# A gated-recurrence layer on one core: the first score matmuls of each head in the middle of a weight piece, and operands 128 bytes lower

## The chip, the cores and the metric

The kernel runs on one core of a Trainium2 chip. The metric is the device time of one execution in microseconds (us). The core has five engines with instruction streams of their own: TensorE (PE: matmuls; its weight loads are listed as PEld), VectorE (DVE), ScalarE (ACT), GpSimd (POOL) and SyncE (SP, which issues most DMAs). They meet through semaphores only: an instruction may wait until a counter has a value, and may raise one when it ends.

## What is computed

One layer of a streaming encoder, for a prompt of 2048 frames and a sample of 64 frames with a state carried in; the model width is 1024. Layer 0 is the only layer, so of the four token mixers only HGRN2 (a gated linear recurrence) runs, followed by a SwiGLU channel mixer, each behind an RMSNorm and added to its input:

```python
def _gla_chunk(state, q, k, v, logf):          # one chunk of 64 frames of one head, 8 heads of 128
    G = jnp.cumsum(logf, axis=2)
    g_mid = G[:, :, L // 2][:, :, None]
    g_last = G[:, :, L - 1][:, :, None]
    scores = jnp.einsum('bhtd,bhsd->bhts', q * jnp.exp(G - g_mid), k * jnp.exp(g_mid - G))
    scores = jnp.where(tril, scores, 0.0)
    o = scores @ v + jnp.einsum('bhtd,bhdv->bhtv', q * jnp.exp(G), state)
    new_state = exp(g_last).T * state + einsum('bhsd,bhsv->bhdv', k * jnp.exp(g_last - G), v)

def _hgrn2(h, layer, state, w_in, lower_bounds, out_gain, w_out):
    q, f, i, g = jnp.split(h @ w_in, ...)      # 1024 -> 4 x 1024
    fg = lb + (1.0 - lb) * sigmoid(f); k = 1.0 - fg; logf = log(fg); v = i
    o, state = _chunked_scan(_gla_chunk, ...)
    o = _rmsnorm(o, out_gain)
    return (o * silu(g)) @ w_out, state

x = x + _hgrn2(rmsnorm(x)); x = x + (silu(gate) * up) @ w_down     # gate, up: 1024 -> 2816 each
```

## The kernel before

**Tiling.** The 2048 frames go through in four blocks. Block 0 has 512 prompt frames and the 64 sample frames (576, handled as two halves of 288 columns); blocks 1 to 3 have 512. Block 0 is written out, blocks 1 to 3 are one loop. All activations stand with the features on the 128 partitions and the frames along the row. Every large product is made of three matmuls on a high and a low part of each operand (`w_hi*h_hi + w_hi*h_lo + w_lo*h_hi`, lines 452 to 454 in `products`).

**A block** has three stages. (1) The eight heads: for each, q, f, i and g are projected from `h_hi`, `h_lo` by eight weight *pieces* of four 128-row tiles, that is 4 x 3 = 12 matmuls of 512 columns to a piece. (2) The output projection, from the heads' results `a_hi`, `a_lo`. (3) The SwiGLU: gate and up by a Strassen scheme (for each of 22 tiles seven operands, A11, S2, S3, S1, A22, A12, S4 in that order, of 4 x 3 matmuls of 256 columns: 1848 a block, 5544 in blocks 1 to 3; `strassen`, lines 544 to 546), and down, again from `a_hi`, `a_lo`, which by then hold the SwiGLU's products (22 x 8 x 3 = 528 matmuls of 512 columns a block, 1584 in blocks 1 to 3; the output projection has 576 there).

**Weights** arrive in a ring of four buffers, three pieces ahead. For each piece ACT makes `w_hi` (line 761) and DVE `w_lo` (line 941, `split_lo`), once the piece that used the buffer has been multiplied.

**The recurrence of head h-1 is woven into head h's pieces.** Behind piece u of head h, every engine runs its `recurrence(b, h - 1, u)`. A block's 512 frames are four *pairs* of chunks, p = 0 to 3. PE's steps are: `turn_values` (u = 0: v transposed into `ps_u`), `scores` of pair u into `ps_s`, `turn_keys` of pair u into `ps_k`, `update` of pair u-1 (state update), `outputs` of pair u-2. On the other engines: `keep_scores` (DVE, lines 964 and 965: two masked copies from `ps_s` to `sc`), `keys_by_frame` (ACT, line 662: `ps_k` to `kx`), `next_states` (DVE, line 988), `first_state` (DVE, line 973: `smid`).

**What waits for what.** There is one bank `ps_s` and one bank `ps_k`. So the scores of pair p wait until pair p-1 has been copied out:

```python
wait(pe, sc_ready, pair_no(b, h, p))      # in scores: for p > 0, behind keep_scores(p - 1)
pe.wait_ge(kx_ready, pair_no(b, h, p) + 1)     # in update(p): behind keys_by_frame(p)
```

The first pair's scores wait for q and k with their decays, of which `qe` (DVE, line 1108) is written last before them; `turn_keys(0)` waits for `kh` (line 1113). At each boundary between two heads, DVE also finishes an older head's output: `oscale` (line 996), `y` (line 1000), then ACT rounds it to `a_hi` (line 694, `y_part`), then DVE takes the rest as `a_lo` (line 1009, `y_part`). DVE runs in the order it is written in, with `y_part` behind `recurrence(b, h - 1, 0)` and ahead of the next `split_lo`. The boundary behind the first head of a block has no `y_part`. The eighth head's recurrence is woven into the first pieces of the output projection (`last_head`).

So a block has 8 places where a head's recurrence begins: a first one, six with `y_part`, and that of `last_head`.

**Addresses.** `place` hands out bytes of each partition in the order of the calls. `h_hi` begins at byte 16512, `h_lo` at 34944, `w_hi` at 107648, `w_lo` at 115840; then come small tables, of which `coef` (3 numbers for each of 4 pairs) is the last, and the next address is rounded up to 128. There `a_hi` begins, at 148992; `a_lo` at 167424, the gate and up weights `g_hi` at 200192 and `g_lo` at 214528, and behind them the scratch tensors of the heads that lie over these. The Strassen operands of the activations (`h2`, at 16512) have slots of 1152 bytes; with the weights' slots of 2048 bytes, an operand's address less its weight's leaves, modulo 512: 0 for A11 and S2, 128 for S3 and A12, 256 for A22 and S4, 384 for S1 (for the high parts). For `h_hi` less `w_hi` it leaves 0 modulo 128 and 0 modulo 256 (16512 - 107648 = -356 x 256); for `a_hi` less `w_hi` it leaves 128 modulo 256.

Of the kernel before, what the change touches and what calls it, by code (L numbers as in the profile page):

```python
# [19 lines left out]
P = 128  # L20
EPS = 1e-6
D = 1024
KT = D // P
HEADS = 8
# [35 lines left out]
PAIRS = TB // P  # L60
# [3 lines left out]
def hybrid_layer(nc, x_t, w_all, gain_mix, gain_ffn, bounds, out_gain, state_in, y_t, state_p, state_s,  # L64
# [3 lines left out]
    at = [-(-nc.sbuf_base // 32) * 32]  # L68

    def place(name, shape, dt=F32, offset=None):  # L70
        here = at[0] if offset is None else offset
        size = 4
        for n in shape[1:]:
            size *= n
        size = (size + 31) // 32 * 32
        if offset is None:
            at[0] += size
        return nc.alloc_sbuf_tensor_at(name, shape, dt, offset=here), here + size
# [22 lines left out]
    fbuf, _ = place("fbuf", [P, 2, T0])  # L101
    gmix, _ = place("gmix", [P, KT])
    gffn, _ = place("gffn", [P, KT])
    bnd, _ = place("bnd", [P, 2, HEADS])
    bexp, _ = place("bexp", [P, 2, HEADS])
    bmax, _ = place("bmax", [P, HEADS])
    bsum, _ = place("bsum", [P, HEADS])
# [3 lines left out]
    ogain, _ = place("ogain", [P, 1])  # L111
    eps, _ = place("eps", [P, 1])
    e_mid, _ = place("e_mid", [P, 2 * PAIRS + 2])
    coef, _ = place("coef", [P, PAIRS, 3])

    at[0] = -(-at[0] // P) * P
    a_at = at[0]
# [174 lines left out]
    with nc.Block() as block:  # L292

        @block.tensor
        def _(pe):
# [83 lines left out]
            def out_square_sum(b, h):  # L379
                if isinstance(h, int) and h == HEADS - 1:  # L380
                    pe.wait_ge(osq_ready, HEADS * b + h + 1)
                    mm = pe.matmul(ps_s[:, 0:TB], ones[:], osq[:, 0:TB], start=True, stop=True)
                    if first(b):
                        mm = pe.matmul(ps_k[:, 0:CH], ones[:], osq[:, TB:T0], start=True, stop=True)
                    mm.then_inc(oms_done, 1)
                    return
                pe.wait_ge(osq_lo_ready, HEADS * b + h + 1)
                pe.matmul(ps_s[:, 0:TB], ones_r[:], osq_hi[:, 0:TB], start=True, stop=False)
                mm = pe.matmul(ps_s[:, 0:TB], ones_r[:], osq_lo[:, 0:TB], start=False, stop=True)
                if first(b):  # L390
                    pe.matmul(ps_k[:, 0:CH], ones_r[:], osq_hi[:, TB:T0], start=True, stop=False)
                    mm = pe.matmul(ps_k[:, 0:CH], ones_r[:], osq_lo[:, TB:T0], start=False, stop=True)
                mm.then_inc(oms_done, 1)

            def recurrence(b, h, u):

                n = pairs_of(b)
                if u == 0:
                    turn_values(b, h)
                if u == VS_STEP and first(b):  # L400
                    turn_sample_values(b, h)
                if 0 <= u - 2 < n:
                    outputs(b, h, u - 2)
                if 0 <= u - 1 < n:
                    update(b, h, u - 1)
                if u < n:
                    scores(b, h, u)
                    turn_keys(b, h, u)
                if u == P_HEAD - 1:
                    out_square_sum(b, h)  # L410

            def slot_read(b, h, t, recur):

# [17 lines left out]
            def head(b, T, h, recur):  # L431

                for u in range(P_HEAD):
                    t, half = u // 2, u % 2
                    if not recur:
                        t, half = ((0, 0), (1, 0), (0, 1), (1, 1), (2, 0), (2, 1), (3, 0), (3, 1))[u]
                    if half == 0:
                        slot_read(b, h, t, recur)
                    piece(b, T, slot(b, t), P_HEAD * h + u, u % RING, half, KT, h_hi, h_lo,
                          KT * b if u in (0, 2) and not recur else None)  # L440
                    if recur:
                        recurrence(b, h - 1, u)
                    elif u == (2 if first(b) else 3):
                        norm_sum(b, T, 2 * b)
# [3 lines left out]
            def products(T, s, ring, kk, k, stop, part_hi, part_lo):  # L448
                for bank, c, n in halves(T):
                    o = ps[s % 2][:, s // 2 + bank, 0:n]  # L450
                    hh, hl = part_hi[:, k, c:c + n], part_lo[:, k, c:c + n]
                    pe.matmul(o, w_hi[:, ring, kk, :], hh, start=(k == 0), stop=False)  # L452
                    pe.matmul(o, w_hi[:, ring, kk, :], hl, start=False, stop=False)  # L453
                    last_mm[0] = pe.matmul(o, w_lo[:, ring, kk, :], hh, start=False, stop=stop)  # L454

            def piece(b, T, s, n, ring, j, tiles, part_hi, part_lo, part_wait=None):

                pe.wait_ge(w_lo_ready, PIECES * b + n + 1)
                for kk in range(min(KP, tiles - j * KP)):
                    k = j * KP + kk  # L460
                    if part_wait is not None:
                        pe.wait_ge(h_lo_ready, part_wait + k + 1)
                    products(T, s, ring, kk, k, k == tiles - 1, part_hi, part_lo)
                last_mm[0].then_inc(pieces_done, 1)

            def last_head(b, T):


                h = HEADS - 1


                pieces = ((0, 0), (1, 0), (0, 1), (1, 1), (2, 0), (3, 0))
                parts = [(n, m, KP * half + kk) for n, (m, half) in enumerate(pieces) for kk in range(KP)
                         if KP * half + kk < h and (m < 2 or not first(b))]
                share = (4, 1, 1, 1, 1, 1, 1, 1) if first(b) else (4, 2, 2, 2, 2, 1, 0, 1)
                for u in range(P_HEAD + 1):
                    take = share[u] if u < len(share) else len(parts)
                    for n, m, k in parts[:take]:
                        if k % KP == 0:
                            pe.wait_ge(w_lo_ready, PIECES * b + OUT0 + n + 1)  # L480
                        if k == 0:
                            if first(b):
                                pe.wait_ge((v_t_ready, qe_ready)[m], HEADS * (b + 1))
                            else:
                                pe.wait_ge((f_norm_ready, g_norm_ready, v_t_ready, qe_ready)[m], HEADS * (b + 1))
                        if n == 0 and k == 0:
                            pe.wait_ge(y_lo_ready, HEADS * b + h - 1)
                        if n == 2 and k == h - 1:
                            pe.wait_ge(y_lo_ready, HEADS * b + h)
                        products(T, slot(b, m), n % RING, k % KP, k, False, a_hi, a_lo)  # L490
                        if n < 2 and k == KP - 1:
                            last_mm[0].then_inc(pieces_done, 1)
                    parts = parts[take:]
                    if u < P_HEAD:
                        recurrence(b, h, u)
                pe.wait_ge(y_lo_ready, HEADS * (b + 1))
                for m in range(2):
                    products(T, slot(b, m), 2 + m, KP - 1, KT - 1, True, a_hi, a_lo)

                    last_mm[0].then_inc(pieces_done, 1 if first(b) or m == 0 else 3)  # L500
# [123 lines left out]
        def _(act):  # L624
# [71 lines left out]
            def recurrence(b, h, u):  # L696
                n = pairs_of(b)
                if u == 0:
                    values_by_frame(b, h)
                if u == VS_STEP and first(b):  # L700
                    sample_values_by_frame(b, h)
                if u < n:
                    keys_by_frame(b, h, u)
                if u == n + 1:
                    out_squares(b, h)
# [230 lines left out]
        def _(dve):  # L936
# [74 lines left out]
            def recurrence(b, h, u):  # L1011
                n = pairs_of(b)
                if u == 0:
                    first_state(b, h)
                if 0 <= u - 1 < n:
                    next_states(b, h, u - 1)
                if u < n:
                    keep_scores(b, h, u)
                if u == P_HEAD - 2 and (first(b) or (isinstance(h, int) and h == HEADS - 1)):
                    low_squares(b, h)  # L1020
# [311 lines left out]
            dve.wait_ge(x1_ready, 2)  # L1332
            nc.vector.tensor_copy(ones_r[:], ones[:]).then_inc(dve_const, 1)
            nc.vector.memset(e_mid[:, 2 * PAIRS:2 * PAIRS + 1], 1.0).then_inc(dve_const, 1)
            nc.vector.memset(coef[:, :, 2:3], 1.0).then_inc(dve_const, 1)
            dve.wait_ge(dve_const, 4)
            dve.wait_ge(dn_done, 2)
            for s in range(2):
                dve.wait_ge(y_stored[s], 1)
# [21 lines left out]
            nc.vector.tensor_scalar(oml[:], lb[:], -1.0, 1.0, ALU.mult, ALU.add).then_inc(bound_ready, 1)  # L1361
            dve.wait_ge(bound_step, 7)
            dve.wait_ge(bound_ready, 1)
            dve.wait_ge(smp_loaded, 16)
            block_program(0, T0)
            with dve.Fori(1, BLOCKS) as b:
# [335 lines left out]
```

## Time and profile before

| | |
|---|---|
| median of 3 runs | 2655.53 us (2654.55 to 2661.32) |
| the profiled execution | 2655.65 us; its span from first to last instruction 2653.9 us |
| granted TensorE clock, mean | 0.993 of full speed |
| busy: PE, DVE, ACT, POOL | 2579.9, 1795.3, 1237.2, 259.9 us |

A busy engine executes something; PE's busy time and the durations of its matmuls overlap (a matmul starts before the one ahead of it has drained), so what a matmul costs is read from start to start. The engine with the largest share sets the time as long as the others deliver to it in time; where it stands idle, the trace names what ended the wait.

### The profile page before, as it was taken

How to read it: one execution, taken by the hardware profiler on the slowest of the kernel's cores; microseconds unless marked ns; L12 is line 12 of the kernel's file. 1: busy time of each engine (PE TensorE's matmuls, PEld its weight loads, DVE VectorE, ACT ScalarE, POOL GpSimd, SP SyncE). 2: the span in 40 equal slices, each digit the busy share in tenths (PEclk: the TensorE clock that was granted, in tenths of full speed). 3: DMA queues.
4: the chain of work that ended last, by engine and by line, in shares of the span. 5: the costliest groups of instructions: out<-in, count | busy, mean ns of one | idle time of the engine just before them, and what ended most of it. 6: DMA issues, size and time to landing. Idle time of an engine off the chain costs nothing.

```text
span 2653.9 us, 52582 instructions
## 1 busy us (share of the span) xinstructions
PE 2579.9 (97%) x16420; PEld 2339.6 (88%) x16420; DVE 1795.3 (68%) x3025; ACT 1237.2 (47%) x2195; POOL 259.9 (10%) x196
## 2 busy tenths in 40 slices
PE   8999989999999999999999999999999999999998
PEld 7999989999988887998987887889897888799897
DVE  6666587877756677766656676766565676766565
ACT  5444454433444555443435555534344554644343
POOL 3111110000021112000011111100002111200001
PEclk9999999999999999999999999999999999999999
DMA  5322345645542224765753222667554222467574
GB/s 183 96 59 59 112 139 175 205 162 178 175 142 76 71 75 127 215 210 161 217 154 96 71 75 88 208 181 226 155 178 144 72 75 73 150 198 223 153 224 140
DMA packets 203408, 379.63 MB, mean 143 GB/s; under 512 B 23168, under 2 KB 23200, under 8 KB 203056
## 3 DMA queue, kind: packets, MB, share of 16 engines
q1 hardware_dynamic: 202896, 369.73, 45.1%
q0 software_dynamic: 384, 8.44, 0.9%
q8 instruction: 50, 0.82, 0.1%
q14 instruction: 78, 0.64, 0.1%
HBM read 331.67 MB, written 52.74 MB: 145 GB/s over the span
## 4 chain that ended last, share of the span: by engine, by line
PE 56%; DVE 8%; issue 6%; ACT 5%; DMA 0%; DVEq 0%; ACTq 0%; SPq 0%; POOL 0%; POOLq 0%
PE ps L452 9%; PE ps L454 9%; PE ps L453 9%; PE ps L544 8%; PE ps L546 8%; PE ps L545 8%; DVE w_lo L941 2%; PE ps_s L330 1%; PE ps_s L544 1%; PE ps_s L545 1%; PE ps_s L546 1%; ACT L729 1%; DVE gcum L1037 1%; ACT w_hi L761 1%; DVE coef L1093 1%
## 5 line engine op out<-in xcount | busy, mean ns | idle before, releaser
L544 PE MATMUL ps<-h,g_hi 128*128 128x256 f32 (+1 forms) x2112 | 608.8, 288 | 29.8 <-DVE xres L1131 9.7
L546 PE MATMUL ps<-h,g_lo 128*128 128x256 f32 (+1 forms) x2112 | 604.5, 286 | 0.0
L545 PE MATMUL ps<-h,g_hi 128*128 128x256 f32 (+1 forms) x2112 | 604.2, 286 | 0.0
L941 DVE TENSOR_TENSOR w_lo<-w_raw,w_hi 128x512 fp32r<-128x512 f32 x512 | 370.2, 725 | 235.8 <-ACT w_hi L761 234.4
L452 PE MATMUL ps<-h_hi,w_hi 128*128 128x512 f32 (+1 forms) x1280 | 470.9, 368 | 15.8 <-DVE h_lo L946 10.6
L761 ACT ACTIVATE w_hi<-w_raw 128x512 fp32r<-128x512 f32 x512 | 317.1, 624 | 334.7 <-PE ps L454 319.0
L454 PE MATMUL ps<-h_hi,w_lo 128*128 128x512 f32 (+1 forms) x1280 | 453.0, 354 | 0.0
L453 PE MATMUL ps<-h_lo,w_hi 128*128 128x512 f32 (+1 forms) x1280 | 451.8, 353 | 0.0
L452 PE MATMUL ps<-a_hi,w_hi 128*128 128x512 f32 (+1 forms) x1200 | 432.9, 361 | 6.1 <-DVE w_lo L941 3.5
L544 PEld LDWEIGHTS ps<-h,g_hi 128*128 128x128 f32 x2112 | 402.1, 190 | 40.3 <-DVE ebuf L1251 15.8
L453 PE MATMUL ps<-a_lo,w_hi 128*128 128x512 f32 (+1 forms) x1200 | 426.5, 355 | 0.0
L454 PE MATMUL ps<-a_hi,w_lo 128*128 128x512 f32 (+1 forms) x1200 | 425.8, 355 | 0.0
L545 PEld LDWEIGHTS ps<-h,g_hi 128*128 128x128 f32 x2112 | 402.3, 190 | 0.4
L546 PEld LDWEIGHTS ps<-h,g_lo 128*128 128x128 f32 x2112 | 401.7, 190 | 0.0
L452 PEld LDWEIGHTS ps<-h_hi,w_hi 128*128 128x128 f32 x1280 | 243.8, 190 | 49.4 <-issue 9.0
L454 PEld LDWEIGHTS ps<-h_hi,w_lo 128*128 128x128 f32 x1280 | 241.7, 189 | 31.7
L1382 POOL TENSOR_TENSOR ssq<-ssq,ebuf 128x512 f32<-128x512 f32 (+1 forms) x72 | 113.6, 1578 | 1593.0 <-ACT ebuf L641 1591.4
L452 PEld LDWEIGHTS ps<-a_hi,w_hi 128*128 128x128 f32 x1200 | 226.3, 189 | 46.2 <-DVE w_lo L941 8.1
L453 PEld LDWEIGHTS ps<-h_lo,w_hi 128*128 128x128 f32 x1280 | 242.4, 189 | 26.6 <-issue 0.7
L454 PEld LDWEIGHTS ps<-a_hi,w_lo 128*128 128x128 f32 x1200 | 226.6, 189 | 31.9
L453 PEld LDWEIGHTS ps<-a_lo,w_hi 128*128 128x128 f32 x1200 | 226.5, 189 | 30.3 <-issue 0.7
L821 ACT ACTIVATE g_hi<-g_raw 128x512 fp32r<-128x512 f32 x264 | 164.7, 625 | 133.6 <-PE ps L546 133.2
(179 smaller groups left out, 3601.7 us busy)
## 6 DMA issues: line engine op xcount, KB each, us to landing
w_raw<-w_all SPq DMA_DIRECT2D x516, 256.0 KB, 2.7
g_raw<-w_all SPq DMA_DIRECT2D x286, 256.0 KB, 3.6
g_x<-kept_sum SPq DMA_DIRECT2D x132, 256.0 KB, 3.6
g_hi<-kept_hi SPq DMA_DIRECT2D x132, 256.0 KB, 2.9
g_lo<-kept_lo SPq DMA_DIRECT2D x132, 256.0 KB, 3.1
kept_sum<-g_x SPq DMA_DIRECT2D x44, 256.0 KB, 3.0
kept_hi<-g_hi SPq DMA_DIRECT2D x44, 256.0 KB, 2.4
kept_lo<-g_lo SPq DMA_DIRECT2D x44, 256.0 KB, 2.5
```

What stands on the lines that cost most here:

```text
L330: mm = pe.matmul(ps_s[:, 0:3 * CH], ke[:, p * P:(p + 1) * P], qe[:, p * 3 * CH:(p + 1) * 3 * CH], start=True, stop=True)
L452: pe.matmul(o, w_hi[:, ring, kk, :], hh, start=(k == 0), stop=False)
L453: pe.matmul(o, w_hi[:, ring, kk, :], hl, start=False, stop=False)
L454: last_mm[0] = pe.matmul(o, w_lo[:, ring, kk, :], hh, start=False, stop=stop)
L544: pe.matmul(out, g_hi[:, o, k, :].bitcast(F32R), hh, start=(k == 0 and not more), stop=False, skip_group_check=True)
L545: pe.matmul(out, g_hi[:, o, k, :].bitcast(F32R), hl, start=False, stop=False, skip_group_check=True)
L546: mm = pe.matmul(out, g_lo[:, o, k, :].bitcast(F32R), hh, start=False, stop=last, skip_group_check=True)
L729: act.preload_act_table_set("natural_log_exp_and_others")
L761: nc.scalar.activation(w_hi[:, r, :, :], w_raw[:, r, :, :], ACT.Copy).then_inc(w_hi_ready, 1)
L821: nc.scalar.activation(g_hi[:, o].bitcast(F32R), operand_of(o), ACT.Copy).then_inc(g_hi_ready, 1)
L941: nc.vector.tensor_tensor(w_lo[:, r, :, :], w_raw[:, r, :, :], w_hi[:, r, :, :].bitcast(F32), ALU.subtract).then_inc(w_lo_ready, 1)
L1382: nc.gpsimd.tensor_tensor(ssq[:, 0:T], ssq[:, 0:T], ebuf[:, s, 0:T], ALU.add).then_inc(ssq_ready, 1)
```

## The change

Two things change. First, the scores and the key transposition of a head's first pair no longer stand right behind `turn_values`, but in the middle of the next piece, behind its second tile (`first_pair`, called by `piece` through `between`). On DVE `keep_scores(0)` and on ACT `keys_by_frame(0)` move from step u = 0 to step u = 1, and so behind `y_part` and behind the split of the next piece's weights. In the eighth head all three stay at u = 0. Second, `coef` is laid over `bnd`, a table that only the start of the program reads; its memset moves from DVE's first instructions to the end of the bound's computation. With `coef` gone from the end of the tables, all that is placed behind them begins 128 bytes lower: `a_hi` at 148864, `a_lo` at 167296, `g_hi` at 200064, `g_lo` at 214400. No DMA is added, dropped or moved in its queue.

```diff
+    bnd_at = at[0]
     bnd, _ = place("bnd", [P, 2, HEADS])
+    coef, _ = place("coef", [P, PAIRS, 3], offset=bnd_at)
...
     e_mid, _ = place("e_mid", [P, 2 * PAIRS + 2])
-    coef, _ = place("coef", [P, PAIRS, 3])
...
                     update(b, h, u - 1)
-                if u < n:
+                if 0 < u < n:
                     scores(b, h, u)
                     turn_keys(b, h, u)
                 if u == P_HEAD - 1:
                     out_square_sum(b, h)
+
+            def first_pair(b, h):
+                scores(b, h, 0)
+                turn_keys(b, h, 0)
...
-                          KT * b if u in (0, 2) and not recur else None)
+                          KT * b if u in (0, 2) and not recur else None,
+                          (lambda: first_pair(b, h - 1)) if u == 1 and recur else None)
...
                     products(T, s, ring, kk, k, k == tiles - 1, part_hi, part_lo)
+                    if between is not None and kk == 1:
+                        between()
...
                     if u < P_HEAD:
                         recurrence(b, h, u)
+                    if u == 0:
+                        first_pair(b, h)
...
-                if u < n:
+                if u == (0 if isinstance(h, int) and h == HEADS - 1 else 1):
+                    keys_by_frame(b, h, 0)
+                if 0 < u < n:
                     keys_by_frame(b, h, u)
...
                     first_state(b, h)
+                if u == (0 if isinstance(h, int) and h == HEADS - 1 else 1):
+                    keep_scores(b, h, 0)
                 if 0 <= u - 1 < n:
                     next_states(b, h, u - 1)
-                if u < n:
+                if 0 < u < n:
                     keep_scores(b, h, u)
...
-            nc.vector.memset(coef[:, :, 2:3], 1.0).then_inc(dve_const, 1)
-            dve.wait_ge(dve_const, 4)
...
             dve.wait_ge(bound_ready, 1)
+            nc.vector.memset(coef[:, :, 2:3], 1.0).then_inc(dve_const, 1)
+            dve.wait_ge(dve_const, 4)
```

What this makes of the order at one of the six boundaries with `y_part`, in the loop over blocks 1 to 3. On PE, from the transposition of the values (L309 `ps_u`) on; L330 is `scores`, L345 `turn_keys`, L452 to L454 are the products of the next piece. Before:

```order
L309 MATMUL ps_u<-ident,v_t 128x128 [waits smid_ready]
L309 MATMUL ps_u<-ident,v_t 128x128 x3
L253 ISA [waits qhat_ready,oln_ready,qe_ready,ke_ready]
L330 MATMUL ps_s<-qe,ke 128x192 [waits sc_ready]
L345 MATMUL ps_k<-ident,kh 128x128 [waits kh_ready,kx_ready]
L458 ISA
L452 MATMUL ps<-h_hi,w_hi 128x512 [waits w_lo_ready]
L453 MATMUL ps<-h_lo,w_hi 128x512
L454 MATMUL ps<-h_hi,w_lo 128x512
```

and now (the line numbers have grown by 1 and by 6):

```order
L310 MATMUL ps_u<-ident,v_t 128x128 [waits smid_ready]
L310 MATMUL ps_u<-ident,v_t 128x128 x3
L464 ISA
L458 MATMUL ps<-h_hi,w_hi 128x512 [waits w_lo_ready]
L459 MATMUL ps<-h_lo,w_hi 128x512
L460 MATMUL ps<-h_hi,w_lo 128x512
L458 MATMUL ps<-h_hi,w_hi 128x512
L459 MATMUL ps<-h_lo,w_hi 128x512
L460 MATMUL ps<-h_hi,w_lo 128x512
L254 ISA [waits qhat_ready,oln_ready,qe_ready,ke_ready]
L331 MATMUL ps_s<-qe,ke 128x192 [waits sc_ready]
L346 MATMUL ps_k<-ident,kh 128x128 [waits kh_ready,kx_ready]
```

The wait for `qe` has moved behind six products of the next piece; six more follow it, then the update of pair 0 and the scores of pair 1.

On DVE, at the same boundary, from `first_state` (`smid<-state`) to `next_states` of pair 0 (`smid<-smid`). Before:

```order
L973 TENSOR_SCALAR smid<-state,e_mid 128x128
L951 REGISTER_ALU
L253 REGISTER_ALU [waits scores_done]
L964 COPY_PREDICATED sc<-causal,ps_s 64x128 [waits out_done]
L965 COPY_PREDICATED sc<-causal,ps_s 64x64
L1008 ISA
L1009 ISA [waits y_hi_ready]
L1009 TENSOR_TENSOR a_lo<-y_113,a_hi 128x512
L940 REGISTER_ALU
L941 TENSOR_TENSOR w_lo<-w_raw,w_hi 128x512 [waits w_hi_ready]
L986 REGISTER_ALU [waits update_done]
L988 SCALAR_TENSOR_TENSOR smid<-smid,fac,ps_u 128x128 [waits smid_ready]
```

and now (the line numbers have grown by 12):

```order
L985 TENSOR_SCALAR smid<-state,e_mid 128x128
L1020 ISA
L1021 ISA [waits y_hi_ready]
L1021 TENSOR_TENSOR a_lo<-y_113,a_hi 128x512
L952 REGISTER_ALU
L953 TENSOR_TENSOR w_lo<-w_raw,w_hi 128x512 [waits w_hi_ready]
L963 REGISTER_ALU
L254 REGISTER_ALU [waits scores_done]
L976 COPY_PREDICATED sc<-causal,ps_s 64x128 [waits out_done]
L977 COPY_PREDICATED sc<-causal,ps_s 64x64
L998 REGISTER_ALU [waits update_done]
L1000 SCALAR_TENSOR_TENSOR smid<-smid,fac,ps_u 128x128 [waits smid_ready]
```

The two copies of `keep_scores(0)` now stand behind `a_lo`, which waits for ACT's `a_hi`, and behind the next `w_lo`, which waits for ACT's `w_hi`.

On ACT, from the copy of the values on (`y_113` is `y`). Before:

```order
L652 ACTIVATE v_tok<-ps_u 128x512 [waits v_turned]
L660 ISA
L662 ACTIVATE kx<-ps_k 128x128 [waits update_done,k_turned]
L693 ISA
L694 ISA [waits y32_ready]
L694 ACTIVATE a_hi<-y_113 128x512
L759 ISA
L253 REGISTER_ALU [waits w_loaded0]
L761 ACTIVATE w_hi<-w_raw 128x512 [waits pieces_done]
```

and now:

```order
L662 ACTIVATE v_tok<-ps_u 128x512 [waits v_turned]
L703 ISA
L704 ISA [waits y32_ready]
L704 ACTIVATE a_hi<-y_113 128x512
L771 ISA
L254 REGISTER_ALU [waits w_loaded0]
L773 ACTIVATE w_hi<-w_raw 128x512 [waits pieces_done]
L670 ISA
L672 ACTIVATE kx<-ps_k 128x128 [waits update_done,k_turned]
```

`kx` of pair 0 has moved behind `a_hi` and the next `w_hi`.

## Rows read from the trace of the kernel before

**Rows 1.** The page's first part: busy time, share, instructions of each engine.

```profile
PE 2579.9 (97%) x16420; PEld 2339.6 (88%) x16420; DVE 1795.3 (68%) x3025; ACT 1237.2 (47%) x2195; POOL 259.9 (10%) x196
```

**Rows 2.** Groups by form, PE: count, busy us, mean ns, idle before, releasers.

```profile
L452 PE MATMUL ps<-a_hi,w_hi 128*128 128x512 f32 x720 | 288.8, 401 | 3.5 <-DVE w_lo L941 3.5
...
L330 PE MATMUL ps_s<-qe,ke 128*128 128x192 f32 x192 | 49.8, 341 | 12.6 <-DVE qe L1108 12.6
```

**Rows 3.** Timeline of PE at a boundary with `y_part`: start, duration, [idle before].

```profile
2104.26 0.59 PE L330 MATMUL ps_s<-qe,ke 128*128 128x192 f32 x2 [0.43 <-DVE qe L1108]
...
2107.82 0.49 PE L330 MATMUL ps_s<-qe,ke 128*128 128x192 f32 x2
...
2108.18 0.48 PE L452 MATMUL ps<-h_hi,w_hi 128*128 128x512 f32 x1
```

**Rows 4.** Timeline of DVE at the same boundary.

```profile
2106.53 0.29 DVE L964 COPY_PREDICATED sc<-causal,ps_s 64x128 f32<-64x128 uint32 x1
2106.84 0.23 DVE L965 COPY_PREDICATED sc<-causal,ps_s 64x64 f32<-64x64 uint32 x1
2107.10 0.69 DVE L1009 TENSOR_TENSOR a_lo<-y,a_hi 128x512 f32 x1
2107.71 0.68 DVE L941 TENSOR_TENSOR w_lo<-w_raw,w_hi 128x512 fp32r<-128x512 f32 x1
```

**Rows 5.** Timeline of ACT at the same boundary.

```profile
2105.96 0.63 ACT L694 ACTIVATE a_hi<-y 128x512 f32 x1 [0.68 <-DVE y L1000]
2106.49 0.61 ACT L761 ACTIVATE w_hi<-w_raw 128x512 fp32r<-128x512 f32 x1
```

**Rows 6.** Timeline of DVE in a `last_head`, block 1.

```profile
993.59 0.24 DVE L965 COPY_PREDICATED sc<-causal,ps_s 64x64 f32<-64x64 uint32 x1
```

**Rows 7.** Timeline of PE in that `last_head`.

```profile
993.88 0.59 PE L330 MATMUL ps_s<-qe,ke 128*128 128x192 f32 x2
...
994.34 0.48 PE L452 MATMUL ps<-a_hi,w_hi 128*128 128x512 f32 x1
```

**Rows 8.** Timeline of PE at block 1's first boundary.

```profile
795.25 0.59 PE L330 MATMUL ps_s<-qe,ke 128*128 128x192 f32 x2 [1.52 <-DVE qe L1108]
...
798.63 0.38 PE L355 MATMUL ps_u<-v_tok,kx 128*128 128x128 f32 x2
```

**Rows 9.** Timeline of DVE at block 1's first boundary.

```profile
796.03 0.28 DVE L973 TENSOR_SCALAR smid<-state,e_mid 128x128 f32<-128x128 f32 x1
```

**Rows 10.** Timeline of ACT at a boundary with `y_part` in block 0.

```profile
119.38 0.69 ACT L694 ACTIVATE a_hi<-y 128x576 f32 x1 [0.54 <-DVE y L1002]
```

**Rows 11.** Timeline of DVE at that boundary of block 0.

```profile
120.53 0.76 DVE L1009 TENSOR_TENSOR a_lo<-y,a_hi 128x576 f32 x1
```

**Rows 12.** Timeline of PE at that boundary of block 0.

```profile
121.77 0.39 PE L326 MATMUL ps_s<-qe,ke 128*128 128x128 f32 x2
```

**Rows 13.** Timeline of PE, block 1: head products without a break (18 rows).

```profile
815.03 0.39 PE L452 MATMUL ps<-h_hi,w_hi 128*128 128x512 f32 x1
...
818.88 0.39 PE L454 MATMUL ps<-h_hi,w_lo 128*128 128x512 f32 x1
```

**Rows 14.** Timeline of PE, block 1: down products without a break (55 rows).

```profile
1130.22 0.39 PE L452 MATMUL ps<-a_hi,w_hi 128*128 128x512 f32 x1
...
1142.76 0.40 PE L452 MATMUL ps<-a_hi,w_hi 128*128 128x512 f32 x1
```

**Rows 15.** Timeline of PE, gate and up: first rows of S1, A22, A11, S3, S1.

```profile
1291.85 0.28 PE L544 MATMUL ps<-h,g_hi 128*128 128x256 f32 x1
...
1293.29 0.28 PE L544 MATMUL ps<-h,g_hi 128*128 128x256 f32 x1
...
1297.53 0.28 PE L544 MATMUL ps<-h,g_hi 128*128 128x256 f32 x1
...
1300.33 0.28 PE L544 MATMUL ps<-h,g_hi 128*128 128x256 f32 x1
...
1301.76 0.28 PE L544 MATMUL ps<-h,g_hi 128*128 128x256 f32 x1
```

More of the change, by code:

```diff
@@ L454, in products, with piece @@
                     last_mm[0] = pe.matmul(o, w_lo[:, ring, kk, :], hh, start=False, stop=stop)
-            def piece(b, T, s, n, ring, j, tiles, part_hi, part_lo, part_wait=None):
+            def piece(b, T, s, n, ring, j, tiles, part_hi, part_lo, part_wait=None, between=None):
                 pe.wait_ge(w_lo_ready, PIECES * b + n + 1)
```

## The prediction

> **What bounds the kernel now.** I read the page's busy times first: PE is busy for 97% of the span, DVE for 68% and ACT for 47% [rows 1]. So a change counts only through what PE executes, how densely it does so, and where it waits. The groups by form show next where PE waits in the code that moves: the first scores of a head wait for DVE's `qe` in 24 places of blocks 1 to 3, 12.6 us in all [rows 2]. The timelines at three kinds of boundary [rows 3 to 12] give the chains on PE, DVE and ACT there. Last, the start-to-start times of matmuls in unbroken runs [rows 13 to 15] show that the same matmul does not have one price. Head products of 512 columns follow each other at 3.85 us / 17 = 226.5 ns [rows 13], down products of 512 columns at 12.54 / 54 = 232.2 ns [rows 14].
>
> **The scores, at the six boundaries with `y_part` (18 in blocks 1 to 3).** PE's wait of 0.43 us for `qe` [rows 3] goes, since six products stand ahead of it now. What is late next is the second scores. They need `ps_s` copied out by `keep_scores(0)`, and this is now queued on DVE behind `a_lo` and `w_lo`. Step by step at the boundary shown: `a_hi` begins at 2105.96 and takes 0.63, so it ends at 2106.59 [rows 5]. DVE is free at 2106.53, where the copies stood [rows 4]; so `a_lo` begins at 2106.62, when `a_hi` has been seen. From `a_lo` to `w_lo` it takes 0.61 (2107.10 to 2107.71, [rows 4]), so `w_lo` begins at 2107.23; its own `w_hi` has ended at 2106.49 + 0.61 = 2107.10 [rows 5] and does not delay it. Of the same size as `a_lo`, `w_lo` takes 0.61 too: the copies begin at 2107.84 and end 0.54 later (2106.53 to 2106.84 + 0.23, [rows 4]), at 2108.38. That scores wait for this copy is seen once in the program before, in `last_head`: the copy ends at 993.59 + 0.24 = 993.83 [rows 6], the scores begin at 993.88 and the next products at 994.34 [rows 7], that is 0.05 and 0.46 later. So the products that began at 2108.18 [rows 3] begin at 2108.38 + 0.05 + 0.46 = 2108.89: 0.71 later, after a wait of about 1.0 us in place of 0.43. PE can do nothing else meanwhile, since the rest of its program stands behind the scores. Nothing later gives it back: the next head's chain starts from PE's own projections, which are as much later. 18 x 0.71 = **+12.8 us**.
>
> `kx(0)`, moved behind `a_hi` and `w_hi` on ACT, begins when `w_hi` ends, about 2107.10, and takes some 0.2; the update of pair 0, which waits for it, would be reached at 2107.2. It is up to 0.1 late, but the scores behind it are held for 1 us by the copy, which covers this.
>
> **The first boundary (3 in blocks 1 to 3).** No `y_part` stands here, and PE waits 1.52 us for `qe` [rows 8]. Six products move ahead of that wait, so everything behind is earlier by 6 x 0.2265 = 1.36 us, if no new wait arises. The update moves from 798.63 [rows 8] to 797.27, and the second scores to 797.49. On DVE, `smid` begins at 796.03 [rows 9]; 0.19 behind it `w_lo` at 796.22, the copies 0.61 later at 796.83, ended at 797.37, seen at 797.42: in time by 0.07. 3 x -1.36 = **-4.1 us**. If the copies come 0.3 later than worked out, it is -3.4.
>
> **Block 0 (6 boundaries).** Here PE had no wait. `a_hi` ends at 119.38 + 0.69 = 120.07 [rows 10]; `a_lo` at 120.10 takes 0.67 to the next start (0.76 busy [rows 11] less the overlap of 0.08 seen in blocks 1 to 3: 0.69 busy, 0.61 to the next); `w_lo` 120.77, copies 121.38 to 121.92, seen at 121.97. The second scores began at 121.77 [rows 12], so they are 0.20 later, up to 0.30 with the drained pipeline behind a wait (0.46 to the products instead of 0.36 [rows 3, 7]). 6 x 0.25 = **+1.5 us**.
>
> **The memset.** It has no row here that I use; the smallest DVE row, a copy of 64x64, takes 0.23 [rows 4], so it lies between 0 and 0.2, and I take **+0.1 us**: the computation of the bound stands at the start, where block 0 waits for its tables. No DMA is issued elsewhere, and POOL's and SP's queues are not passed.
>
> **The addresses.** The trace cannot show what the shift does, only how matmul prices differ between operands whose addresses differ. The head products' activations lie a multiple of 256 bytes from their weights, at 226.5 ns; the `a_hi` and `a_lo` products' lie 128 off, at 232.2. The shift gives the latter the distance of the former. If the distance is the cause, 1584 down products gain 5.7 ns each, **-9.0 us**. The 576 of the output projection would gain 3.3; but PE waits 3.5 us for `w_lo` in that group already [rows 2], so I count half, **-1.6 us**. In block 0 (288 columns) I found no such difference and count nothing.
>
> The 5544 gate and up matmuls of blocks 1 to 3 change class too. S1 (remainder 384) takes 1.44 / 12 = 120.0 ns, A22, A12 and S4 (256, 128, 256) together 4.24 / 36 = 117.8, A11 and S2 (0) 2.80 / 24 = 116.7, S3 (128) 1.43 / 12 = 119.2 [rows 15]. All move 128 up, S1 to 0. With 118.1 for the classes 128 and 256 (117.8 three times, 119.2 once): S3 and A12 stay within these, A11 and S2 lose 1.4 each, S4 and A22 lose 1.9 each, S1 gains 3.3; 3.3 / 7 = 0.47 ns, **+2.6 us**. The bounds are all at the cheapest (a mean of 118.0 falls to 116.7: -7 us) and all at the dearest (to 120.0: +11 us).
>
> [...]
>
> **The sum:** 12.8 - 4.1 + 1.5 + 0.1 - 9.0 - 1.6 + 2.6 = +2.3 us on the profiled execution's 2655.65, which is the median of the runs shown within 0.12: **2657.9 us**. What a measurement of this kernel tells from no change is 0.3%, 8 us, so this is "the same".
>
> **Rivals.** (A) Slower: the dearer price of the down products belongs to their stage (what else reads memory then), not to the distance of addresses. Then only the scheduling is left, 12.8 - 4.1 + 1.5 + 0.1 = +10.3: 2665.9 us. It decides as soon as less than a quarter of the 10.6 us arrives. For it: prices differ across stages whose traffic differs. Against it: the head products run beside a DVE and an ACT that are as busy, and their 226.5 is regular over 17 gaps, as if locked. [...] (B) The gate and up products fall to the cheapest class: -7 instead of +2.6, 2648.3 us. For it: a spread of 3.3 ns on 5544 matmuls. Against it: at least S1's neighbours have to move against what their classes show. (C) They rise towards S1's 120.0: +11, 2666.3 us, slower. (D) Faster: the second scores never wait, since DVE reaches the copies earlier than worked out. Then 18 boundaries save 0.43 instead of losing 0.71, 20.5 us less: 2637.4. It needs the copies done by 2107.4 instead of 2108.4, that is ahead of `a_lo` and `w_lo`, and DVE runs in order.
>
> **Chances.** Forecast (2653 to 2663) 0.49, A 0.16, B 0.11, C 0.08, D 0.06; a longer wait than worked out, by 0.3 us and more at each of 18 boundaries (2663 and above), 0.05; a gain on the addresses beyond the sum (output projection in full, block 0 as well) 0.05. The range from 2647 to 2666.5 leaves out D and the far ends of the others, 0.2 together. Faster by over 0.3% (below 2647.6): D, half of B, a little of the last, 0.14. Slower (above 2663.6): A, C and the longer wait, 0.27. The same: 0.59.
>
> **What would show it.** Right: PE's idle time ahead of the second scores (L331), released by DVE's second copy, about 1 us at each of 18 boundaries; none ahead of the first scores; `kx` of pair 0 behind `w_hi`; 1.36 us gained at the first boundary of blocks 1 to 3; down products 226.5 ns apart; S1's price near 116.7 and that of A11, S2, A22 and S4 higher. Wrong: down products still at 232 (A), gate and up all moved one way (B, C), or no idle time ahead of L331's second scores (D).

## The result and the profile after

The changed kernel takes 2661.67 us (median of 11 runs, 2658.5 to 2664.43), the kernel before, in the same sessions, 2654.86 (11 runs, 2652.01 to 2661.32). The ratio is 1.002, with a 95% interval from 1.0012 to 1.0028: 5.3 us slower (3.2 to 7.4; the two medians lie 6.8 apart). That lies within the 0.3% that I called "the same", and within the range; the sum had said +2.3. The profiled execution has a span of 2662.4 us, 8.5 more than before.

The waits of the changed kernel, PE's and its weight loads' (total us, number, longest), and the groups by form that answer to [rows 2]:

```profile
PEld ps_s L331 <- DVE sc L977: 16.8, 18, 0.9
...
PE ps_s L331 <- DVE sc L977: 13.3, 18, 0.8
...
PEld ps_u L356 <- ACT kx L672: 12.4, 18, 0.7
```

```profile
L458 PE MATMUL ps<-a_hi,w_hi 128*128 128x512 f32 x720 | 285.2, 396 | 4.8 <-DVE w_lo L953 4.5
...
L356 PE MATMUL ps_u<-v_tok,kx 128*128 128x128 f32 x256 | 52.6, 287 | 4.7 <-ACT kx L672 4.7
L331 PE MATMUL ps_s<-qe,ke 128*128 128x192 f32 x192 | 49.9, 341 | 14.5 <-DVE sc L977 13.3 <-DVE qe L1122 1.0
```

The wait for `qe` has all but gone (12.6 to 1.0 us). In its place stand exactly 18 waits for the second of DVE's two copies, 13.3 us, and 18 smaller ones of the update for `kx`, 4.7 us. The timeline of PE at the boundary that answers to [rows 3] shows both:

```profile
2110.60 0.60 PE L310 MATMUL ps_u<-ident,v_t 128*128 128x128 f32 x4
...
2112.43 0.48 PE L331 MATMUL ps_s<-qe,ke 128*128 128x192 f32 x2
...
2114.68 0.49 PE L356 MATMUL ps_u<-v_tok,kx 128*128 128x128 f32 x2 [0.26 <-ACT kx L672]
2115.90 0.59 PE L331 MATMUL ps_s<-qe,ke 128*128 128x192 f32 x2 [0.73 <-DVE sc L977]
...
2116.36 0.47 PE L458 MATMUL ps<-h_hi,w_hi 128*128 128x512 f32 x1
```

The first scores now start without a wait. The second start at 2115.90, 5.30 us behind the transposition of the values; before, it was 4.59 (2107.82 less 2103.23). The bracketed idle time, 0.73, undercounts the stall, since it is counted from the end of the update (0.49 long here), while in the kernel before the scores started 0.21 behind the start of an update of 0.38: between the starts of update and scores lie 1.22 us, where it was 0.21 (2107.82 less 2107.61). The two rows of the kernel before that this is counted from:

```profile
2103.23 0.60 PE L309 MATMUL ps_u<-ident,v_t 128*128 128x128 f32 x4
...
2107.61 0.38 PE L355 MATMUL ps_u<-v_tok,kx 128*128 128x128 f32 x2
```

DVE and ACT of the changed kernel at the same place, answering to [rows 4] and [rows 5]:

```profile
2114.11 0.69 DVE L1021 TENSOR_TENSOR a_lo<-y,a_hi 128x512 f32 x1
2114.72 0.68 DVE L953 TENSOR_TENSOR w_lo<-w_raw,w_hi 128x512 fp32r<-128x512 f32 x1
2115.32 0.28 DVE L976 COPY_PREDICATED sc<-causal,ps_s 64x128 f32<-64x128 uint32 x1
2115.62 0.23 DVE L977 COPY_PREDICATED sc<-causal,ps_s 64x64 f32<-64x64 uint32 x1
```

```profile
2113.31 0.63 ACT L704 ACTIVATE a_hi<-y 128x512 f32 x1 [1.48 <-DVE y L1012]
2113.85 0.62 ACT L773 ACTIVATE w_hi<-w_raw 128x512 fp32r<-128x512 f32 x1
2114.37 0.26 ACT L672 ACTIVATE kx<-ps_k 128x128 f32<-128x128 f32 x1
```

The chain runs as written out: `a_hi` ends at 2113.94, `a_lo` starts at 2114.11, `w_lo` 0.61 and the copies 1.21 later; they end at 2115.85, and the scores start 0.05 behind that. The one step that differs is the first: 0.17 us from the end of `a_hi` to the start of `a_lo`, where I had put 0.03.

The down products, answering to [rows 14], 55 rows:

```profile
1137.53 0.39 PE L458 MATMUL ps<-a_hi,w_hi 128*128 128x512 f32 x1
...
1149.77 0.39 PE L458 MATMUL ps<-a_hi,w_hi 128*128 128x512 f32 x1
```

12.24 / 54 = 226.7 ns, against 232.2 before. Gate and up, answering to [rows 15], the first rows of A11, S3, S1, A22, S4 and the next A11:

```profile
1180.98 0.28 PE L554 MATMUL ps<-h,g_hi 128*128 128x256 f32 x1
...
1183.86 0.28 PE L554 MATMUL ps<-h,g_hi 128*128 128x256 f32 x1
...
1185.27 0.28 PE L554 MATMUL ps<-h,g_hi 128*128 128x256 f32 x1
...
1186.69 0.28 PE L554 MATMUL ps<-h,g_hi 128*128 128x256 f32 x1
...
1189.51 0.28 PE L554 MATMUL ps<-h,g_hi 128*128 128x256 f32 x1
...
1190.94 0.28 PE L554 MATMUL ps<-h,g_hi 128*128 128x256 f32 x1
```

A tile's seven operands take 9.96 us, 118.6 ns each; before it was 9.91 (1301.76 less 1291.85 in [rows 15]), 118.0. A11 and S2 rose from 116.7 to 120.0, S3 and S1 fell to 117.5 and 118.3, A22 and A12 stand at 117.5, S4 at 119.2. That is one tile. Over the 48 tiles of the six full groups of blocks 1 to 3 the mean goes from 118.0 to 118.6: A11 from 116.7 to 119.7, S2 from 116.7 to 119.8, S3 from 119.0 to 118.0, S1 from 119.9 to 117.8, A22 from 118.1 to 117.3, A12 from 117.3 to 118.3, S4 from 118.2 to 119.2.

The plainest reading of the heads is the time from one head's transposition of the values to the next (mean over the six heads that begin with a `y_part` boundary, blocks 1 to 3; five in block 0; one for the first head), worked out from the starts of the rows of L309 or L310 in each trace:

| kernel | blocks 1 to 3 | block 0 | first head of blocks 1, 2, 3 |
|---|---|---|---|
| before | 28.05, 28.06, 28.06 | 35.08 | 29.17, 29.17, 29.16 |
| changed | 28.81, 28.81, 28.82 | 35.52 | 27.75, 27.75, 27.27 |
| address alone | 27.94, 27.94, 27.94 | 35.14 | 29.13, 29.08, 29.09 |
| order alone | 28.92, 28.91, 28.91 | 35.50 | 27.90, 27.84, 27.86 |
| copies and kx first | 27.45, 27.47, 27.45 | 35.11 | 27.64, 27.68, 27.68 |
| copies between | 28.22, 28.22, 28.21 | 35.11 | 27.65, 27.65, 27.66 |
| copies first, kx late | 27.79, 27.80, 27.80 | 35.11 | 27.67, 27.67, 27.63 |
| kx first, copies late | 28.80, 28.81, 28.81 | 36.48 | 28.49, 28.49, 28.50 |
| gate and up back | 28.90, 28.90, 28.90 | 35.51 | 27.89, 27.86, 27.86 |
| weights up | 28.94, 28.95, 28.94 | 35.54 | 27.92, 28.14, 28.08 |
| copies first, gate and up back | 27.54, 27.55, 27.55 | 35.06 | 27.74, 27.71, 27.76 |
| copies first, weights up | 27.67, 27.69, 27.67 | 35.10 | 27.83, 28.00, 27.97 |

### The profile page after: what moved, and what is told of

It reads as the page before. It is cut to its first block, busy times and chain, and to the rows that moved or that the text cites. A ratio compares the mean times of both kernels' runs of the same rounds, so it can differ in the third digit from the quotient of the medians.

```text
span 2662.4 us, 52588 instructions
## 1 busy us (share of the span) xinstructions
PE 2580.0 (97%) x16420; PEld 2343.4 (88%) x16420; DVE 1795.6 (67%) x3025; ACT 1233.8 (46%) x2195; POOL 260.1 (10%) x196
## 4 chain that ended last, share of the span: by engine, by line
PE 53%; DVE 9%; issue 6%; ACT 5%; DMA 1%; DVEq 1%; ACTq 0%; SPq 0%; POOL 0%; POOLq 0%
PE ps L458 8%; PE ps L460 8%; PE ps L459 8%; PE ps L554 8%; PE ps L555 7%; PE ps L556 7%; DVE w_lo L953 2%; PE ps_s L556 1%; PE ps_s L554 1%; PE ps_s L555 1%; PE ps_s L331 1%; ACT L741 1%; DVE gcum L1051 1%; ACT w_hi L773 1%; ACT logf L744 1%
```

## Experiments

Two theories stood against each other at first. Mine: the terms of the sum are real and add up; the place of the copies in DVE's queue costs some 12 us, and the address pays most of it back. The rival: the address is worth nothing, and the 5 us are what the order costs. All kernels were timed in 5 rounds or more against the kernel before on the same chip.

**The address alone.** The kernel before, with this and no more:

```diff
+    bnd_at = at[0]
     bnd, _ = place("bnd", [P, 2, HEADS])
+    coef, _ = place("coef", [P, PAIRS, 3], offset=bnd_at)
...
-    coef, _ = place("coef", [P, PAIRS, 3])
...
-            nc.vector.memset(coef[:, :, 2:3], 1.0).then_inc(dve_const, 1)
-            dve.wait_ge(dve_const, 4)
...
             dve.wait_ge(bound_ready, 1)
+            nc.vector.memset(coef[:, :, 2:3], 1.0).then_inc(dve_const, 1)
+            dve.wait_ge(dve_const, 4)
```

> The kernel before with the address part alone (coef over bnd, memset moved). Theory 1, the terms add up: down products 226.7 ns apart instead of 232.4 (1584 of them, -9.1 us), output projection -1.1, gate and up +0.58 ns on 5544 (+3.2), start -0.1: 7 us faster than before. Rival: the down gain is given back in the waits around the stages, since ACT and DVE set the pace there: within 2 us of before.

Measured: 2646.32 us against 2656.04, ratio 0.9959 (0.9945 to 0.9972), some 11 us faster. The rival falls. It is more than the 7 expected; 2 us of that are the heads, which gain 0.12 each (28.06 to 27.94), and the rest lies within the interval (7 to 15 us).

**The order alone.** The changed kernel with the old addresses:

```diff
-    coef, _ = place("coef", [P, PAIRS, 3], offset=bnd_at)
...
     e_mid, _ = place("e_mid", [P, 2 * PAIRS + 2])
+    coef, _ = place("coef", [P, PAIRS, 3])
```

> The changed kernel with coef back at the end of the tables, so that all addresses are those of before and only the order differs. Theory 1: 18 boundaries at +0.77 (+13.9), block 0 six at +0.44 (+2.6), three first boundaries at -1.4 (-4.2): 12 us slower than before, 7 slower than the changed kernel. Rival, the address part is worthless and the order costs all of it: 5 us slower than before, as the changed kernel.

Measured: 2669.38 against 2656.04, ratio 1.0051 (1.0038 to 1.0065), 13.5 us slower. A boundary costs 0.86 us (28.06 to 28.91), a first head gains 1.30 (29.17 to 27.87), block 0 loses 0.42 a head: 18 x 0.86 - 3 x 1.30 + 6 x 0.42 = +14.1. The two halves, -11 and +13.5, add up to the change's +5.3 within their intervals.

**The copies and `kx` first.** PE's part of the change stays, DVE's and ACT's are undone:

```diff
-                if u == (0 if isinstance(h, int) and h == HEADS - 1 else 1):
-                    keys_by_frame(b, h, 0)
-                if 0 < u < n:
+                if u < n:
                     keys_by_frame(b, h, u)
...
-                if u == (0 if isinstance(h, int) and h == HEADS - 1 else 1):
+                if u == 0:
                     keep_scores(b, h, 0)
```

> The changed kernel with keep_scores(0) on DVE and keys_by_frame(0) on ACT back at step u = 0, ahead of a_lo, a_hi and the next weights; PE's scores and key transposition stay in the middle of the piece. Theory 1, the place in DVE's queue makes the wait of the second scores: the wait goes, each of 18 boundaries saves 0.43 against before instead of losing 0.77, block 0 loses nothing, the first boundaries keep -1.4: with the address part 19 us faster than before (-7.7 -4.5 -7.1). Rival, something else holds the second scores (kx, the update, or DVE too full between two heads): the gain stops at the address part and the first boundaries, 11 us faster or less.

Measured: 2632.9 against 2656.04, ratio 0.9919 (0.9905 to 0.9932), 21.5 us faster than before and so faster than both kernels. PE's timeline at a boundary of this kernel:

```profile
847.68 0.60 PE L310 MATMUL ps_u<-ident,v_t 128*128 128x128 f32 x4
...
849.52 0.48 PE L331 MATMUL ps_s<-qe,ke 128*128 128x192 f32 x2
...
851.34 0.38 PE L356 MATMUL ps_u<-v_tok,kx 128*128 128x128 f32 x2
...
851.57 0.59 PE L331 MATMUL ps_s<-qe,ke 128*128 128x192 f32 x2
```

The long wait is gone: the second scores start 3.89 us behind the transposition instead of 5.30. A short one is left. The second copy and the list of waits:

```profile
851.28 0.23 DVE L975 COPY_PREDICATED sc<-causal,ps_s 64x64 f32<-64x64 uint32 x1
```

```profile
PEld ps_s L331 <- DVE sc L975: 1.3, 6, 0.3
```

Here, too, the scores start about 0.05 behind the end of the copy (851.57 against 851.51), and so they do at all 18 boundaries. At 12 of them that is no later than the update lets them (3.88 to 3.90 behind the transposition), at the other six they come 0.2 later (4.05 to 4.11). So DVE still sets the second scores, as the rival's last case has it, but by 0.2 us at a third of the boundaries. The scores in the middle of the piece are worth about 0.5 us a head (27.94 with the address alone, 27.45 here), as long as DVE and ACT keep their old order.

**The copies between `a_lo` and `w_lo`.** A smaller dose of the same cause:

```diff
-                if u == (0 if isinstance(h, int) and h == HEADS - 1 else 1):
+                if u == 0 and isinstance(h, int) and h == HEADS - 1:
                     keep_scores(b, h, 0)
...
                         y_part(b, T, h - 2)
+                    if u == 0 and recur:
+                        keep_scores(b, h - 1, 0)
```

> The changed kernel with keep_scores(0) on DVE behind a_lo, but ahead of the next w_lo; ACT as in the change. Theory 1: the copies come one w_lo, 0.61 us, earlier, so a boundary costs 0.16 instead of 0.77 in blocks 1 to 3 (+2.9 against before in all) and nothing in block 0; with -4.5 and -7.1 it is 9 us faster than before. Rival, a_lo's wait for a_hi is the whole delay, or the update's wait for kx takes over: within 4 us of the changed kernel.

Measured: 2645.9 against 2656.04, ratio 0.9962 (0.9948 to 0.9975), 10 us faster. One `w_lo` fewer ahead of the copies takes 0.60 us off each head (28.81 to 28.22), which is the 0.61 from one start to the next: dose and response agree.

**`kx` and the copies apart.** Two kernels undo one half each; first the copies alone, then `kx` alone:

```diff
-                if u == (0 if isinstance(h, int) and h == HEADS - 1 else 1):
+                if u == 0:
                     keep_scores(b, h, 0)
```

> The changed kernel with keep_scores(0) on DVE back at u = 0; keys_by_frame(0) on ACT stays behind a_hi and w_hi. Theory 1: the wait of the second scores goes, and the update's wait for kx, 0.4 us, which it covered, comes to light: 18 x 0.4 = 7 us slower than the version with both first, about 15 us faster than before. Rival, ACT's place costs nothing: as the version with both first, 23 us faster than before.

```diff
-                if u == (0 if isinstance(h, int) and h == HEADS - 1 else 1):
-                    keys_by_frame(b, h, 0)
-                if 0 < u < n:
+                if u < n:
                     keys_by_frame(b, h, u)
```

> The changed kernel with keys_by_frame(0) on ACT back at u = 0; keep_scores(0) on DVE stays behind a_lo and w_lo. Theory 1: only the update's wait goes, the second scores still wait for the copy: within 2 us of the changed kernel, 5 us slower than before. Rival, ACT's place is the cause: 7 to 14 us faster than the changed kernel.

Copies first: 2640.27 against 2655.92, ratio 0.9938 (0.9925 to 0.9952), 16.5 us faster. Each head is 0.35 longer than with both first: the update's wait for `kx` costs 18 x 0.35 = 6.3 us when nothing covers it, and in the changed kernel it costs nothing, because the wait for the copies lies behind it. `kx` first: 2668.26, ratio 1.0043 (1.003 to 1.0057), 11 us slower than before and 6 slower than the changed kernel. In blocks 1 to 3 that is what I expected (28.81 as in the changed kernel). What I had not seen is block 0, 36.48 instead of 35.52 a head. ACT, DVE and PE there, in this kernel:

```profile
120.96 0.28 ACT L672 ACTIVATE kx<-ps_k 128x128 f32<-128x128 f32 x1 [1.73 <-PE ps_k L346]
121.13 0.68 ACT L704 ACTIVATE a_hi<-y 128x576 f32 x1
```

```profile
121.98 0.76 DVE L1019 TENSOR_TENSOR a_lo<-y,a_hi 128x576 f32 x1 [1.15 <-ACT a_hi L704]
```

```profile
123.84 0.49 PE L327 MATMUL ps_s<-qe,ke 128*128 128x128 f32 x2 [1.11 <-DVE sc L975]
```

`kx` waits for a transposition that now comes late; `a_hi` is queued behind it, `a_lo` waits for `a_hi`, and the copies stand behind `a_lo`. So 6 x 0.96 = 5.8 us; the first heads of blocks 1 to 3 are 0.7 longer too (28.49): there the next `w_hi` is queued behind the late `kx`, `w_lo` waits 0.60 for it in block 1, and the copies stand behind `w_lo`. With the copies ahead of `a_lo` the same late `a_hi` costs nothing (35.11).

**Which distance counts.** In the changed kernel 128 bytes were left free, once ahead of the gate and up weights, once ahead of `w_hi`:

```diff
+    at[0] += P
     g_at = at[0]
```

> The changed kernel with 128 bytes left free ahead of the gate and up weights, so that these (and all behind them) are where they were before, and only a_hi and a_lo stay 128 lower. Theory 1, the price of a product depends on where its two operands lie to each other: gate and up fall back by 0.58 ns each on 5544 to 118.0, 3.2 us faster than the changed kernel; down stays at 226.7. Rival, gate and up's 118.6 comes from the faster down stage or from the order: no difference to the changed kernel.

```diff
+    at[0] += P
     w_hi, _ = place("w_hi", [P, RING, KP, P], F32R)
```

> The changed kernel with 128 bytes left free ahead of w_hi: w_hi, w_lo and all behind them, a_hi, a_lo and the gate and up weights too, lie 128 bytes higher. Theory 1a, the distance between activations and weights counts: head products, now 128 off, go to 232 ns (2304 of them, +13), down stays at 226.7, gate and up fall back to 118.0 (-3): 10 us slower than the changed kernel. Theory 1b, the activations' own address counts (h_hi at 128, a_hi back at 0 modulo 256): head products stay at 226.5, down goes back to 232.4 (+10), gate and up -3 or nothing: 7 to 10 us slower, told apart by the spacing in the trace. Rival, neither counts: as the changed kernel.

Gate and up back: 2660.32 against 2655.86, ratio 1.0015 (1.0006 to 1.0024), not told apart from the changed kernel's 1.002. In the trace gate and up do fall back to 118.0 ns (each of the six full groups of eight tiles 0.39 us shorter than in the changed kernel), but what lies over and behind these weights, the heads' scratch tensors among it, is back too, and each head is 0.09 longer: 18 x 0.09 = 1.6 of the 3.3 gained. Weights up: ratio 1.0018 (1.0009 to 1.0027). The spacing decides between the two readings. Head products of this kernel, 18 rows, and down products, 56 rows:

```profile
843.23 0.40 PE L460 MATMUL ps<-h_lo,w_hi 128*128 128x512 f32 x1
...
847.19 0.39 PE L459 MATMUL ps<-h_hi,w_hi 128*128 128x512 f32 x1
```

```profile
1134.26 0.39 PE L459 MATMUL ps<-a_hi,w_hi 128*128 128x512 f32 x1
...
1146.73 0.39 PE L460 MATMUL ps<-a_lo,w_hi 128*128 128x512 f32 x1
```

Head products take 3.96 / 17 = 232.9 ns now, down products 12.47 / 55 = 226.7. `h_hi` has not moved and `a_hi` stands where it stood in the kernel before: in these long runs the price goes with the distance between activations and weights, 232.2 and 232.9 ns where it is 128 off a multiple of 256, 226.5 and 226.7 where it is a multiple. Yet the 10 us that I expected from it did not come. The heads are only 0.13 longer (28.94 against 28.81), although 96 products at 4 to 5 ns more make 0.4: in the changed kernel the second scores wait for DVE anyway, and part of the longer pieces falls into that wait (5.12 us from the transposition to the second scores, instead of 5.30). In the mean over the 18 boundaries the stretch behind the second scores is 0.34 longer, and the scores come 0.21 earlier, since `a_hi`, counted from the transposition, ends 0.21 earlier.

To see that price without the wait, the same 128 bytes in the version with copies and `kx` first, and for the other half of the question the gate and up weights back in that version:

> The version with copies and kx first, with 128 bytes left free ahead of w_hi, so that head products lie 128 off and cost 232 instead of 227 ns. Theory 1, with the refinement that in the changed kernel the dearer head products were hidden in the wait of the second scores: here that wait is gone, so 2304 products at +5 ns show, +11, gate and up -3: about 8 us slower than the version with copies and kx first, 15 us faster than before. Rival, the chain through DVE and ACT sets the pace of a head in any case: within 2 us of that version.

> The changed kernel with keep_scores(0) and keys_by_frame(0) back at u = 0 and the gate and up weights back at their old addresses. Theory 1, the terms add up: 3 us faster than the version with the copies first alone, about 22 us faster than before. Rival: no faster than that version.

Weights up: 2636.97 against 2655.92, ratio 0.9927 (0.9914 to 0.9941). My +8 is not there; the time alone does not tell this version from the one without the 128 bytes (0.9919), as the rival had it. The trace shows why. A head is 0.22 longer (27.45 to 27.68), half of what 96 products make. Behind the second scores it is 0.36 longer (84 products at 4.3 ns); ahead of them the products cost the same in both versions (see the last section), and the short wait for the copies is gone: these end 3.68 us behind the transposition instead of 3.90, the scores start at 3.89 or 3.90 at all 18 boundaries, and the products behind them start 0.14 earlier. So the other half of the heads' price falls into DVE's short wait, too. Gate and up give 3.3 back. Gate and up back: 2632.8 against 2655.86, ratio 0.9913 (0.99 to 0.9927), not told apart from the version without: in the trace the six groups fall by 0.39 each as before, and the heads take 0.09 more each.

## Why the prediction was right, step by step

**The wait that takes the place of the one removed** was there, at the place, in the number and by the releaser that the sum named: 18 times, second scores, second copy. The order alone shows its price, 0.86 instead of 0.71. The 0.14 that was missing is the first step of the chain: `a_lo` is seen to start 0.17 behind the end of `a_hi` (0.16 to 0.18 at all 18 boundaries), not 0.03. In the kernel before `a_lo` never waited for `a_hi` at these boundaries, where it began 0.51 us or more behind the end of `a_hi`, so no row of them showed this delay, and I took a smaller one. Where that kernel's `a_lo` did wait, for the eighth head's `a_hi` (0.70 us in block 1), it began 0.03 behind its end (1008.12 to 1008.15); why the same step takes 0.17 at the boundaries no run shows. The difference makes 18 x 0.14 = 2.5 us, most of what the sum fell short.

**`kx`** was late by 0.26 of PE's idle time, more than the 0.1 that I gave it, and cost nothing, as worked out; the kernel with the copies first shows what it costs without cover, 0.35 a head.

**The first boundaries** gained 1.42 in blocks 1 and 2 (forecast 1.36) without a new wait, though with nothing to spare: in block 1 the copies end at 800.53, and the second scores start at 800.58. In block 3 it was 1.89 in this profile, but that head began later, and in the kernel with the order alone it is 1.27 to 1.33 in all three.

**Block 0** lost 0.44 a head instead of 0.25, again mostly by the 0.14 of `a_lo` (it starts at 120.49, `a_hi` ends at 120.32).

**The addresses.** Down gained 5.5 ns on 1584 products, -8.8 us (forecast -9.0); the output projection is some 0.35 us shorter in each block, -1.1 (-1.6); gate and up lost 0.59 ns on 5544, +3.3 (+2.6). Only the mean of the last is right. A22 should have risen with S4 and fell (118.1 to 117.3), A11 and S2 rose more than I had worked out, S1 fell to 117.8 and not near 116.7: the remainder modulo 512 is not the rule, and I have none for 256 columns. What I left out is what lies over and behind the gate and up weights, the heads' scratch tensors among it: it moved as well and takes 0.1 us off each head, -2.0 (0.09 comes back in both kernels with the gate and up weights back). Which of these tensors does it stays open. Rival A, that the dear price belongs to the stage, is refuted by the address alone and by the weights moved up. The spacing in long runs follows the distance: down products at 226.7 ns in the changed kernel and with the weights moved up, against 232.2 before; head products at 232.9 with the weights moved up, against 226.5 before. What in the chip makes it so no run shows.

**The sum as measured:** 18 x 0.86 = +15.5 for the order, -2.0 for the heads' addresses, -3 x 1.4 = -4.2, +2.6 in block 0, -8.8, -1.1, +3.3: +5.3 us, which is the measured +5.3. That it fits to the tenth is luck, since the first boundaries are anything from 1.3 (order alone) to 1.6 (the changed kernel's mean), and the memset's +0.1 cannot be read: the time to the first transposition is 0.2 shorter in the changed kernel, and from 1.2 shorter to 0.4 longer in the others. It is luck as well that the forecast came so close: the order cost 3.8 us more than I had worked out (2.7 at the 18 boundaries, 1.1 in block 0), and the heads' addresses, which I had not seen, gave 2.0 of it back.

The 8.5 between the two profiled spans holds some 3 us more. The granted clock shows where. In these profiles it is 1.00 but for a few stretches of 3 to 10 us at 0.50; leaving out the one at the very end, these add up to 37.5 us in the changed kernel's profile and to 30.7 in that of the kernel before. At half speed 6.8 us more cost up to 3.4, by my estimate. The longest lie in the first gate and up groups of blocks 0 and 1 (367.5 to 377.8 and 1053.6 to 1063.8; before, 366.3 to 373.1 and 1045.5 to 1052.4), which are 1.3 and 2.3 us longer than before; one that the kernel before does not have lies at the start of block 3 (2050.3 to 2053.7), behind a wait of PE for `w_lo` of 1.88 us (before: 1.03). With the address alone the stretches add up to 20.5 us, and the mean clock of the changed kernel's runs was anything from 0.992 to 0.996 (the profiled execution before: 0.993); so I take it for the spread between executions.

## What to carry to other kernels

When an instruction is moved to where its own wait is covered, follow its consumers: here the matmul moved half a piece, its copy on DVE moved behind a subtraction that waits for another engine, and the next matmul waited for that copy. The move itself was worth half a microsecond a head; with the consumers left where they stood, and with the lower addresses, the kernel is 0.8% faster than before, about half of it by the addresses. And a few bytes of placement are an edit of their own: time them alone, for the gain of one stage can hide the loss of another.

## What was not expected

The delay behind the end of another engine's instruction was not one figure: `a_lo` began 0.17 us behind the end of ACT's `a_hi` at the 18 boundaries and 0.03 behind it for the eighth head, while PE's scores began 0.05 behind the end of DVE's copy. And the distance of the operands did not set the price of a 512-column product alone. In long runs it is 226.7 or about 232 ns; but in the piece at a boundary of the changed kernel (PE's timeline again, five rows) products of the cheap distance take 0.93 / 4 = 232 ns as well:

```profile
2113.10 0.40 PE L459 MATMUL ps<-h_lo,w_hi 128*128 128x512 f32 x1
...
2114.03 0.40 PE L460 MATMUL ps<-h_hi,w_lo 128*128 128x512 f32 x1
```

These four gaps average 232 ns over the 18 boundaries of the changed kernel, and 231 with the weights moved up, so in this piece the distance makes no difference. Why stays open.
